# Tile 3's second half of the output projection in two pieces, and the choice of tiles 1 and 2 moved ahead of a placing step

## The reference

```
out = merged @ w_out                       # per token, 1024 x 1024
x   = x + out
xn  = rms_norm(x, norm_ffn_w)
lg  = xn @ router_group + bias             # 4 groups: argmax, softmax
le  = xn @ router_expert + bias            # 4 x 8 experts: top 2 inside the chosen group
y  += combine[:, e] * (silu(xn @ gate[e]) * (xn @ up[e])) @ down[e]      # e = 0 .. 31
x   = x + y ;  y_out = rms_norm(x, norm_final_w)
```

## Time and profile before

| | |
|---|---|
| median of 3 runs | 1097.34 us (1096.82 to 1104.91) |
| the profiled execution, its own time | 1104.38 us |
| its span, first to last instruction | 1102.7 us |
| TensorE busy | 1026.5 us (93% of the span) |
| VectorE busy | 563.3 us (51%) |
| ScalarE busy | 370.2 us (34%) |
| GpSimd busy | 442.2 us (40%) |
| mean DMA rate over the span | 166 GB/s, 182.93 MB |
| mean granted TensorE clock | 0.984 of full speed |

### The profile page before, as it was taken

One profiled execution on the slowest core, in us unless ns is written; L12 is line 12 of the kernel. 1 busy time (PEld: TensorE's weight loads), 2 busy tenths in 40 slices (PEclk: granted clock), 3 DMA queues, 4 the chain that ended last, 5 costly groups with the idle time before them and its releaser, 6 DMA issues. The chain is left out here.

```text
span 1102.7 us, 24970 instructions
## 1 busy us (share of the span) xinstructions
PE 1026.5 (93%) x10513; PEld 777.1 (70%) x10513; DVE 563.3 (51%) x1193; ACT 370.2 (34%) x793; POOL 442.2 (40%) x458
## 2 busy tenths in 40 slices
PE   5999999799999999999999999999998999988885
PEld 5777777588888887888888788884557555545442
DVE  6478777646655553877564446434264322221225
ACT  3344545544555443444334461000111111111113
POOL 7546656145455424877573334520001222221120
PEclk9999999999999999999999999999989999999998
DMA  8022221030000007541134124315968999999985
GB/s 259 1 82 76 82 82 39 1 85 4 4 5 4 4 4 180 175 115 39 28 127 125 54 77 156 114 74 196 422 225 329 407 414 413 417 416 416 410 344 232
DMA packets 85944, 182.93 MB, mean 166 GB/s; under 512 B 9848, under 2 KB 59540, under 8 KB 78154
## 3 DMA queue, kind: packets, MB, share of 16 engines
q1 hardware_dynamic: 79325, 168.59, 42.0%
q0 software_dynamic: 5024, 8.36, 2.1%
q10 hardware_dynamic: 1485, 4.39, 1.0%
HBM read 172.72 MB, written 17.55 MB: 173 GB/s over the span
## 5 line engine op out<-in xcount | busy, mean ns | idle before, releaser
L2886 DVE SCALAR_TENSOR_TENSOR ex_sg<-tl_psA,ex_slot_rs,ex_sg 128x128 f32<-128x128 f32 x32 | 11.2, 351 | 127.5 <-ACT ex_sg L2656 127.3
L2316 POOL DMA_INDIRECT tl_xn<-d_tok,ex_gidx x16 | 16.9, 1053 | 148.3 <-DVEq L2881 84.2
L2321 POOL DMA_INDIRECT d_y<-tl_xn,ex_sidx x32 | 31.9, 997 | 109.6 <-DVE tl_xn L2890 102.8
L264 PE MATMUL psv<-xT,w_sum 128*128 128x260 f32 x256 | 61.6, 384 | 0.8 <-DVE uv_gu L1597 0.6
L226 POOL TENSOR_TENSOR w_sum<-w 128x512 f32<-128x512 f32 x16 | 21.2, 1326 | 94.0 <-PE mg_w L264 93.8
L264 PEld LDWEIGHTS psv<-xT,w_sum 128*128 128x128 f32 x256 | 48.4, 190 | 9.3 <-issue 1.0
L2656 ACT ACTIVATE ex_sg<-tl_psA,ex_slot_rs 128x128 f32<-128x128 f32 x32 | 11.7, 367 | 126.8 <-PE tl_psA L2507 126.8
L1060 PE MATMUL ck_b<-ck_X,ck_V 64*64 64x64 f32 x1280 | 50.1, 222 | 2.6 <-issue 1.6
L264 PE MATMUL rk_ps<-xT,rk_w 128*128 128x260 f32 x208 | 50.1, 384 | 0.0
L264 PE MATMUL rk_ps<-xS,rk_w 128*128 128x260 f32 x200 | 48.6, 386 | 0.0
L1060 PEld LDWEIGHTS ck_b<-ck_X,ck_V 64*64 64x64 f32 x1280 | 43.0, 134 | 3.7 <-issue 3.3
(11 more groups left out here) (642 smaller groups left out, 2821.0 us busy)
## 6 DMA issues: line engine op xcount, KB each, us to landing
wd<-in_moe_w_down SPq DMA_DIRECT2D x13, 1024.0 KB
rk_w<-in_w_in SPq DMA_DIRECT2D x12, 1024.0 KB, 5.4
w_uv<-in_w_in SPq DMA_DIRECT2D x16, 512.0 KB, 5.2
w<-in_w_in SPq DMA_DIRECT2D x8, 1024.0 KB, 5.8
tl_x<-in_moe_w_down SPq DMA_DIRECT2D x8, 1024.0 KB
xT<-in_moe_w_gate SPq DMA_DIRECT2D x5, 1024.0 KB
xT<-in_moe_w_up SPq DMA_DIRECT2D x5, 1024.0 KB
w<-in_proj_a SPq DMA_DIRECT2D x4, 1024.0 KB, 5.4
```

Source lines behind the costliest of these rows:

```text
L264: ins = eng.matmul(bank[:, 0:TH], w[:, k, :], x[:, k, :], start=(first and k == 0), stop=(last and k == NK // 2 - 1), skip_group_check=True)
L2316: eng.indirect_dma_start(out=xg[:, p % 2, :], out_offset=None, in_=m.d_tok, in_offset=bass.IndirectOffsetOnAxis(ap=gidx[:, p:p + 1], axis= ...
L2321: eng.indirect_dma_start(out=m.d_y2, out_offset=bass.IndirectOffsetOnAxis(ap=rows, axis=0), in_=yo[:, x, :], in_offset=None, bounds_check= ...
L2886: eng.scalar_tensor_tensor(out=sg[:, out, :], in0=psg[out][:, P:2 * P], scalar=scale, in1=sg[:, out, :], op0=ALU.mult, op1=ALU.mult).then_ ...
```

## The change

`out_part` gets a third argument: the column halves that it computes. Its signal is given with the last column half alone. TensorE now takes the first column half of tile 3's second part between `scores(1)` and `scores(2)`, and the second column half behind the first ranks. `scores(2)` moves in front of the ranks of tiles 0 and NT. On VectorE `choose(groups[1])`, for tiles 1 and 2, moves in front of `place(0, 2)`. The number of products stays the same.

```
--- before.py
+++ after.py
@@ -2361,15 +2361,16 @@
 
         @code.tensor
         def _(eng):
-            def out_part(j, part):
+            def out_part(j, part, columns=(0, 1)):
                 w = w_parts[part]
-                for h in range(2):
+                for h in columns:
                     for k in range(NK // 2):
                         last = eng.matmul(pso[j % 2][:, h, :], m.mg[:, part * NK // 2 + k, j * P:(j + 1) * P],
                                           w[:, k, h * 512:(h + 1) * 512],
                                           start=(part == 0 and k == 0), stop=(part == 1 and k == NK // 2 - 1),
                                           skip_group_check=(j == 0))
-                last.then_inc((s_lo, s_o)[part], 1)
+                if h == 1:
+                    last.then_inc((s_lo, s_o)[part], 1)
 
             def out_sample():
                 for part, w in enumerate(w_parts):
@@ -2456,12 +2457,13 @@
             turn_tile(2)
             eng.wait_ge(s_lg, 2)
             scores(1)
+            out_part(3, 1, (0,))
+            scores(2).then_inc(s_r, 1)
             eng.wait_ge(s_mb, 1)
             rank_tile(0)
             count_tile(0)
             rank_tile(NT).then_inc(s_rank, 1)
-            scores(2).then_inc(s_r, 1)
-            out_part(3, 1)
+            out_part(3, 1, (1,))
             eng.wait_ge(s_slot, 1)
             count_tile(NT)
             list_tile(0)
@@ -2849,10 +2851,10 @@
             eng.wait_ge(s_sq, 3)
             weighted(2)
             stats(2, 4)
+            eng.wait_ge(s_r, 2)
+            choose(groups[1])
             eng.wait_ge(s_rank, 1)
             place(0, 2)
-            eng.wait_ge(s_r, 2)
-            choose(groups[1])
             add(3)
             weighted(3)
             stats(4, NTT)
```

## The result

| | before | changed |
|---|---|---|
| median of 20 runs each | 1099.78 us (1094.54 to 1107.49) | 1107.93 us (1098.97 to 1113.55) |
| ratio to before, 95% interval | | 1.0047 (1.0027 to 1.0067) |
| the profiled execution, its own time | 1104.38 us | 1104.73 us |
| its span | 1102.7 us | 1103.0 us |
| TensorE busy | 1026.5 us | 1023.0 us |

The changed kernel is slower by 0.47%, which is 5.2 us (3.0 to 7.4) of 1099.78. That is within 1%. The two medians are 8.2 us apart and the two means 6.4, so the ratio on record is the smallest of three measures; how it is formed is not on record, and I go by it because it alone comes with an interval. The two profiled executions alone differ by 0.35 us: single executions of either kernel scatter by some 4 us (standard deviation), so the comparison rests on the 20 runs and the profiles tell only where the time goes inside one execution.

What follows compares the result with a forecast made beforehand. The routing was taken to set the experts' start and so the weight stream's end. `add(3)` 1.2 us earlier, but gathering 2.5 us later at the half clock: 1097.34 + 2.5 = 1099.8 us, range 1094.2 to 1107.4.

Steps and rivals of the forecast that it cites:

- Scores, choice, placing: VectorE after tile 2's scores at 814.91 us: choice 5.50 us and placing 1.20 us in a row, ending at 821.74.
- The new wait and the clock: TensorE stands 2.5 us for the placing, then the clock halves: small matmuls 5.8 us, not 3.16; gathering 2.5 us later.
- The gathering products: Products before the first expert: the half clock costs 1.9 us before and again after, a difference of nothing.
- Expert 7's load: Weight load on SyncE's queue: some 2 to 3 us later, counted from the scores of tile 1.
- Rival A: TensorE, 819.25 to 828 us: clock stays up over the new wait; 1.2 us earlier, 1096.1 us; chance 0.22.
- the term for `add(3)`: VectorE behind choice and placing: `add(3)` starts at 821.8 us instead of 822.99, 1.2 us earlier.
- rival B: Fall at 812 us belongs to the profiled execution alone; change 2.4 us slower at full clock, 1099.7 us; chance 0.08.
- rival C: Nothing arrives at the end, since the stream of expert weights is the bound; 1097.3 us; chance 0.10.
- The earlier loads of experts 5 and 6: Weight loads issued 3.6 us earlier while the DMA engines are idle; costed at nothing.

Runs made afterwards that it cites:

- e3: Changed kernel with three extra 128x512 products, never read, between tile 3's last column half and TensorE's wait for the placing; ratio to before 1.0002 (0.9976 to 1.0027).
- e7: Kernel before, in its own order, with two extra 128x512 products in the waits for ScalarE's copies and VectorE's pick; ratio to before 1.0004 (0.9975 to 1.0034).
- e4: Kernel before with ten extra 128x512 products directly in front of the first expert; ratio to before 1.0063 (1.0036 to 1.0091).
- e2: Changed kernel with VectorE's placing of tiles 0 and NT back in front of its choice of tiles 1 and 2; ratio to before 1.0028 (1.0003 to 1.0053).

## Why the prediction was right, and where it was too small

The direction holds, and so does the chain of reasons from the scores of tile 2 to the gathering; the size was 2.5 us where 5.2 (3.0 to 7.4) was measured. The median of 1107.93 us stands 0.5 us above the upper end of my range, before itself having risen from 1097.34 to 1099.78 with more runs; 1097.34 times the ratio is 1102.5, inside it. That the size is no further off owes something to luck, as the terms show.

**Scores, choice, placing.** I had `add(3)` 13.9 us behind the start of tile 1's scores (821.8 against 807.88 in the timeline); the changed kernel shows 822.54 - 808.79 = 13.75, and the same to 0.01 us in both further executions. The projection at the full clock, the placing as the last step before `add(3)`: as forecast.

**The new wait and the clock.** Forecast 2.5 us, measured 2.25; forecast a fall soon after, scores of 3.4 us and gathering 2.5 us later. The falls came in all three profiles (scores 3.60), but in two of them later than I took it: the work from the first count to the end of the transposes took 3.99, 5.64 and 4.28 us, where the sum has 5.8. Against the execution that the sum was made from, gathering is 0.6, 2.3 and 0.9 us later, not 2.5, and expert 0 is 1.2, 2.6 and 1.2 us later. The gathering products, a difference of nothing in the sum, took 5.98, 5.74 and 5.72 us against 5.42. Expert 7's load, 2 to 3 us later by the forecast, is 1.2 us later. From `add(3)` to expert 0 I had 2.5 + 1.2 = 3.7 us more than before; the three profiles of the changed kernel have 23.3 us on the mean, the five with TensorE's order of before 19.9 (46.50 - 26.20 = 20.3, 20.2, 18.9, 18.9, 21.3), which is 3.4 us more, and 3.0 more than the 20.3 of the execution that the sum was made from. In e3, with the wait filled, it is 18.85 us. Rival A, the clock staying up, happened in none of the three.

**The step that failed is the term for `add(3)`**, "1.2 us earlier". It was made against the one profiled execution, in which the clock fell at 812 us, and against that one it holds (26.20 against 24.84). Over the five executions `add(3)` of before stands at 24.5 us on the mean (22.8 to 26.2), that of the changed kernel at 24.8: 0.3 us later (0.6 with e7), not 1.2 earlier. Where the fall was missing, B's own numbers come close: `add(3)` 2.0 us later (B has 2.4). So rival B was half right; I gave it 0.08 with the words that the stretch of small matmuls is the same in every execution. It is, but the fall behind it is not. The terms as they were measured, 0.3 + 3.4 = 3.7 us at the first expert, lie inside the interval; what makes up the rest, to 5.2 by the ratio or 8.2 by the medians, isn't shown, and eight profiles are too few for it. So two misses went opposite ways: the base of `add(3)` made the forecast too small, the half clock, taken too early for two of the three profiles, made it larger.

**Nothing arrives at the end (rival C)**: does not fit e4. The earlier loads of experts 5 and 6, costed at nothing, came 2.5 us earlier. From 841.5 to 847 us the DMA engines' share is then 0.04 (0.69 before), so the earlier bytes show up as more idle time ahead of expert 7's load, as the sum has it; no run moves these loads alone.

**The rule of the Trainium skill** ("TensorE: Matmul & The Clock Gate", section "Why this matters for your kernels"), by which a short wait passes, gave A's 1096.1. Here it misled: a wait of 2.25 us, and one of 1.37 us in e2, were followed by the half clock each time. That small matmuls and not dense ones came behind them may be the reason; no run put dense ones there. Where 2.6 us of dense work filled the wait, in the one profile of e3, the clock stayed.

## What to carry to other kernels

When dense TensorE work is to hide another engine's work, add up all that this engine has to do before TensorE needs its result: with four products in front of the scores VectorE was done too late and TensorE stood, with one it did not. In this kernel a short wait among small matmuls was followed by 10 us or more at the half clock; work that is thrown away, put into the wait, came out cheaper in the one try (e3). And before a clock fall in one profile is taken as the base of a sum, read a second and a third execution: the same place had it or not.

## What the hardware showed that I had not expected

The same instructions in the same order ran at 0.50, 0.51, 0.79, 1.00, 1.00 and 1.00 of the clock's full rate (mean from 812.0 to 818.6 us) in six executions, behind the same 5 us of transposes, scores and ranks; the 16 matmuls of tile 3's second part took 9.97, 9.80, 8.81, 7.11, 7.11 and 7.11 us. That moves `add(3)` by up to 3.4 us (22.8 to 26.2). How much of the scatter of this kernel it makes is not shown. Among 35 runs of before on one chip the time goes with the mean granted clock (correlation -0.76), but that mean is over the whole execution; and in the fourteen profiles the start of tile 0's scores, ahead of all this, already lies between 793.0 and 799.9 us.
